# Interleaving the first two chunks of the second matrix, a convolution that ends later, and what moves with it

## What is computed

```python
def _conformer_layer(x, norm_g, w_in, dw_w, dw_b, ln_g, ln_b, w_out):
    h = _rms_norm(x, norm_g)
    u = h @ w_in
    a, b, z = jnp.split(u, 3, axis=-1)
    y = a * jax.nn.sigmoid(b)
    y = _depthwise_causal_conv(y, dw_w, dw_b)   # 31 taps
    y = jax.nn.silu(_layer_norm(y, ln_g, ln_b))
    y = y * jax.nn.silu(z)
    return x + y @ w_out
```

## Time and profile before

| | |
|---|---|
| median of 3 runs | 1309.73 us (1308.83 to 1312.35) |
| the profiled execution, its own time | 1308.54 us |
| its span, first to last instruction | 1306.7 us |
| PE busy | 1288.9 us, 99% |
| DVE busy | 827.2 us, 63% |
| ACT busy | 781.7 us, 60% |
| granted clock of TensorE | 0.998 |

### The profile page before, as it was taken

How to read it: one execution, slowest core, us unless ns; L and a number is a source line. 1 busy time by engine, 2 the same in 40 slices (tenths; PEclk the granted TensorE clock), 3 DMA queues, 4 the chain that set the end, 5 groups by cost and what they waited for, 6 DMA issues and landing times.

```text
span 1306.7 us, 16159 instructions
## 1 busy us (share of the span) xinstructions
PE 1288.9 (99%) x5987; PEld 1050.7 (80%) x5987; DVE 827.2 (63%) x1282; ACT 781.7 (60%) x1284; POOL 37.6 (3%) x88
## 2 busy tenths in 40 slices
PE   9999999999999999999999999999999999999997
PEld 7877777677888888888888887889888888888886
DVE  5789999977556665445666666555644445566545
ACT  6599998846547554444455665446845445566543
POOL 1011111100000000000000000000000000000000
PEclk9999999999999999999999999999999999999999
DMA  7599999955666556666554445665655556654563
GB/s 267 155 289 273 302 258 258 280 168 165 184 186 186 186 185 190 194 193 190 164 160 147 146 147 179 186 184 156 182 149 156 161 161 177 190 165 154 179 194 134
DMA packets 124789, 247.54 MB, mean 189 GB/s; under 512 B 7820, under 2 KB 12552, under 8 KB 124552
## 3 DMA queue, kind: packets, MB, share of 16 engines
q1 hardware_dynamic: 119496, 227.63, 55.5%
q0 software_dynamic: 5184, 18.88, 7.4%
q10 hardware_dynamic: 32, 0.01, 0.0%
HBM read 225.51 MB, written 2.10 MB: 174 GB/s over the span
## 4 chain that ended last, share of the span: by engine, by line
PE 88%; ACT 6%; DVE 3%; DMA 2%; issue 1%; SPq 0%; DVEq 0%; ACTq 0%
PE PS L1449 26%; PE PS L1451 26%; PE PS L1450 26%; PE PS L1437 3%; PE PS L1370 3%; ACT tap_products L903 2%; ACT w_hi L487 2%; PE PS L1384 2%; DMA tap_products<-tap_products 1%; ACT L468 1%; DVE w_lo L937 1%; DVE aux L1058 1%; DMA w_raw<-in_a_w_in 1%; DVE heads_out L1261 1%; ACT stage L545 0%
## 5 line engine op out<-in xcount | busy, mean ns | idle before, releaser
L937 DVE TENSOR_TENSOR w_lo<-w_raw,w_hi 128x1024 fp32r<-128x1024 f32 (+2 forms) x406 | 490.3, 1209 | 395.2 <-ACT w_hi L487 393.9
L487 ACT ACTIVATE w_hi<-w_raw 128x1024 fp32r<-128x1024 f32 (+2 forms) x406 | 423.7, 1047 | 401.9 <-PE PS L1451 383.8
L1449 PE MATMUL PS<-w_hi,actA_hi 128*128 128x512 f32 (+1 forms) x856 | 340.8, 398 | 4.5 <-DVE w_lo L937 3.1
L1451 PE MATMUL PS<-w_hi,actA_lo 128*128 128x512 f32 (+1 forms) x856 | 332.1, 388 | 0.0
L1450 PE MATMUL PS<-w_lo,actA_hi 128*128 128x512 f32 (+1 forms) x856 | 331.5, 387 | 0.0
L1449 PE MATMUL PS<-w_hi,actB_hi 128*128 128x512 f32 (+1 forms) x768 | 305.0, 397 | 0.0
L1451 PE MATMUL PS<-w_hi,actB_lo 128*128 128x512 f32 (+1 forms) x768 | 297.3, 387 | 0.0
L1450 PE MATMUL PS<-w_lo,actB_hi 128*128 128x512 f32 (+1 forms) x768 | 296.5, 386 | 0.0
L1449 PEld LDWEIGHTS PS<-w_hi,actA_hi 128*128 128x128 f32 x856 | 160.7, 188 | 41.8 <-issue 8.9
L1450 PEld LDWEIGHTS PS<-w_lo,actA_hi 128*128 128x128 f32 x856 | 160.9, 188 | 34.0 <-issue 3.3
L1451 PEld LDWEIGHTS PS<-w_hi,actA_lo 128*128 128x128 f32 x856 | 160.7, 188 | 32.8
(11 more groups left out here) (235 smaller groups left out, 778.1 us busy)
## 6 DMA issues: line engine op xcount, KB each, us to landing
w_raw<-in_a_w_in SPq DMA_DIRECT2D x96, 512.0 KB, 6.7
w_raw<-in_w_in SPq DMA_DIRECT2D x88, 512.0 KB, 3.7
w_raw<-in_w_kv SPq DMA_DIRECT2D x64, 512.0 KB, 3.8
w_raw<-in_b_w_in SPq DMA_DIRECT2D x64, 512.0 KB, 3.7
tap_products<-tap_products POOLq DMA_DIRECT2D x36, 512.0 KB, 8.1
w_raw<-in_a_w_out SPq DMA_DIRECT2D x32, 512.0 KB, 3.9
w_raw<-in_b_w_out SPq DMA_DIRECT2D x32, 512.0 KB, 3.8
w_raw<-in_w_out SPq DMA_DIRECT2D x32, 512.0 KB, 4.2
```

The costliest lines, as they stand in the source:

```text
L487: nc.scalar.activation(split_slot(u)[0], w_raw[:, RAW_SLOT[u], 0:2 * w], ACT.Copy)\
L937: V.tensor_tensor(wl, w_raw[:, RAW_SLOT[u], 0:2 * w], wh.bitcast(F32), ALU.subtract)\
L1449: T.matmul(bank, ah, wh[:, kk, :], start=first and kk == 0, stop=False)
L1451: ins = T.matmul(bank, al, wh[:, kk, :], start=False, stop=last and kk == 1)
```

## The change

It does these things:

- The first two chunks of the second matrix share units 96 to 111: two units of chunk 12, two of 13, and so on. Quarter g of the input is so first needed by unit 96 + 4g. Chunk 12 is done at unit 110, chunk 13 at 112 (`DONE`, `JUST_DONE`), and their residual sums and transposes move there.
- Ten plain units in place of 17: 21, 35, 46, 53, 55, 64, 76, 82, 87, 89.
- The convolution runs from unit 19 to 89, the transposes for statistics at 43, 62, 77, 90. 37 pairs in place of 36, at other taps; an addition at least 4 steps behind its pair; 5 buffers for sums and 3 for addends, in the room of 4 x 2. The transposes and copies of y are one step earlier.
- Mean and root in step 90, normalisation in 92, 93, 99, 102, the products with silu(z) in 93, 96, 100, 103, with high and low halves one step behind each. Z's third chunk is evacuated in step 89, and the last two wait in the room of y.
- The rotary tables are made in steps 166 to 171.
- The ring of loads is wide from unit 16 on.

```diff
+n = UNITS.index((C_OUT, 0))
+UNITS[n:n + 16] = [(C_OUT + c, 2 * g + i) for g in range(4) for c in range(2) for i in range(2)]
+DONE = [max(u for u, (c, _) in enumerate(UNITS) if c == n) + 1 for n in range(NCH)]
+JUST_DONE = {u: c for c, u in enumerate(DONE)}
...
-WIDE_FROM, WIDE_TO = 20, 100
+WIDE_FROM, WIDE_TO = 16, 100
...
-CONV_FROM = [20, 36, 52, 68]
+CONV_FROM = [19, 35, 51, 67]
...
+PLAIN = {21, 35, 46, 53, 55, 64, 76, 82, 87, 89}
+WHOLE = [u in PLAIN for u in range(NU)]
...
-PAIRS, IN_FLIGHT = 9, 4
+PAIRS, SUMS, ADDENDS = [9, 10, 9, 9], 5, 3
...
-CONV_TO = 88
+CONV_TO = 92
+ACT_LEAD, DVE_LEAD, PAIR_LAG = 0, -5, 4
...
-            if added < len(made) and made[added] + 3 <= u and taken[added // PAIRS]:
+            if added < len(made) and made[added] + PAIR_LAG <= u and taken[j]:
...
-                STATS_AT.append(u + (2 if j == 3 else 4))
+                STATS_AT.append(u + (1 if j == 3 else 4))
...
-MOMENTS_AT = STATS_AT[3] + 1
-NORM_AT = [89, 91, 93, 95]
-Z_EVAC_AT = [73, 80, 93, 96]
-Z_AT = [92, 94, 97, 100]
+MOMENTS_AT = STATS_AT[3]
+NORM_AT = [MOMENTS_AT + at for at in (2, 3, 9, 12)]
+Z_EVAC_AT = [73, 80, 89, 96]
+Z_AT = [93, 96, 100, 103]
+ROPE_AT = FIRST[C_V] + 6
...
         def pair_products(n, i):
-            return tap_products[:, n % IN_FLIGHT, i, :, :]
+            return tap_products[:, SUMS + n % ADDENDS if i else n % SUMS, :, :]
...
+                if u == SQUARES_AT[1] + 1:
+                    want(SIGMOID)
+                if u == ROPE_AT + 3:
                     want(EXP_LN)
...
-                    want(SIGMOID)
+                    table[0] = None
...
-                if s == 4 and 2 <= c <= C_Z and c % 2 == 0:
+                if s == 3 and 2 <= c <= C_Z and c % 2 == 0:
...
+                if u == MOMENTS_AT - 2:
+                    want(EXP_LN)
                 if u == MOMENTS_AT:
                     guess("ln")
+                    want(SILU)
...
-                    if n >= IN_FLIGHT:
-                        act.wait_ge(S["product_added"], n - IN_FLIGHT + 1)
+                    if n >= SUMS:
+                        act.wait_ge(S["product_added"], n - SUMS + 1)
+                    if n >= ADDENDS:
+                        pair_summed(act, n - ADDENDS)
...
-                    gated_parts(f"z{j}", conv, 4 * j, "B", 4 * j,
-                                lambda: dve.wait_ge(S["silu_ready"], j + 1))
+                    transposed(dve, f"z{j}")
+                    dve.wait_ge(S["silu_ready"], j + 1)
+                    for i in range(2):
+                        a = conv[:, 4 * j + 2 * i:4 * j + 2 * i + 2, :]
+                        V.tensor_tensor(a, bank_pair(i), a, ALU.mult).then_inc(S["t_multiplied"], 1)
+                if u - 1 in Z_AT:
+                    j = Z_AT.index(u - 1)
+                    for i in range(2):
+                        hi_bank()
...
+                if C_OUT <= JUST_DONE.get(u, 0) < C_K:
+                    add_residual(JUST_DONE[u], "x1_ready")
...
-                if s == 3 and 2 <= c <= C_Z and c % 2 == 0:
+                if s == 2 and 2 <= c <= C_Z and c % 2 == 0:
```

More of the change, by code:

```diff
@@ L105, in plan_convolution @@
         act_at, dve_at = act_at + ACT_ELSE[u], dve_at + DVE_ELSE[u]
-        while len(made) < 4 * PAIRS and act_at < pe_at:
-            j, m = divmod(len(made), PAIRS)
-            if u < CONV_FROM[j] or len(made) - added >= IN_FLIGHT:
+        while len(made) < PAIR_FROM[4] and act_at < pe_at + ACT_LEAD:
+            j = max(i for i in range(4) if PAIR_FROM[i] <= len(made))
+            if u < CONV_FROM[j] or len(made) - added >= SUMS:
                 break
-            PAIRS_AT[u].append((j, m))
+            PAIRS_AT[u].append((j, len(made) - PAIR_FROM[j]))
             made.append(u)
@@ L113, in plan_convolution @@
         act_at = max(act_at, pe_at - 30)
-        while dve_at < pe_at and added + sum(taken) < 4 * (PAIRS + len(SOLO_TAPS)):
-            if added < len(made) and made[added] + 3 <= u and taken[added // PAIRS]:
-                CONV_OPS[u] += [(added // PAIRS, "add", added % PAIRS, i) for i in (0, 2)]
+        while dve_at < pe_at + DVE_LEAD and added + sum(taken) < PAIR_FROM[4] + sum(len(t) for t in SOLO_TAPS):
+            j = max(i for i in range(4) if PAIR_FROM[i] <= added)
+            if added < len(made) and made[added] + PAIR_LAG <= u and taken[j]:
+                CONV_OPS[u] += [(j, "add", added - PAIR_FROM[j], i) for i in (0, 2)]
                 dve_at, added = dve_at + 12, added + 1
@@ L119, in plan_convolution @@
             open_taps = [i for i in range(4) if u >= CONV_FROM[i]
-                         and taken[i] < len(SOLO_TAPS) - (added < (i + 1) * PAIRS)]
+                         and taken[i] < len(SOLO_TAPS[i]) - (added < PAIR_FROM[i + 1])]
             if not open_taps:
@@ L123, in plan_convolution @@
             j = open_taps[0]
-            CONV_OPS[u] += [(j, "tap" if taken[j] else "first", SOLO_TAPS[taken[j]], k) for k in range(4)]
+            CONV_OPS[u] += [(j, "tap" if taken[j] else "first", SOLO_TAPS[j][taken[j]], k) for k in range(4)]
             dve_at, taken[j] = dve_at + 16, taken[j] + 1
-            if taken[j] == len(SOLO_TAPS):
-                STATS_AT.append(u + (2 if j == 3 else 4))
+            if taken[j] == len(SOLO_TAPS[j]):
+                STATS_AT.append(u + (1 if j == 3 else 4))
         dve_at = max(dve_at, pe_at - 30)
-    assert added == 4 * PAIRS and sum(taken) == 4 * len(SOLO_TAPS), (added, taken)
+    assert added == PAIR_FROM[4] and [len(t) for t in SOLO_TAPS] == taken, (added, taken)
 plan_convolution()
-MOMENTS_AT = STATS_AT[3] + 1
-NORM_AT = [89, 91, 93, 95]
-Z_EVAC_AT = [73, 80, 93, 96]
-Z_AT = [92, 94, 97, 100]
+MOMENTS_AT = STATS_AT[3]
[3 more added lines that the diff above has]
+ROPE_AT = FIRST[C_V] + 6
 SPLITS = []
@@ L667, in _ @@
                         transposed(act, "y3")
[L668 to L672 removed]
+                    if j == 2:
+                        act.wait_ge(S["conv_ready"], 3)
+                    evacuate(C_Z + j, z_stage(j), ACT.Silu, r_x)
+                if u - 1 in Z_AT:
+                    j = Z_AT.index(u - 1)
                     for i in range(2):
@@ L677, in _ @@
                         ins.then_inc(S["t_hi_ready"], 1)
-                if s == 2 and C_OUT < c <= C_K:
-                    j = c - C_OUT - 1
+                if C_OUT <= JUST_DONE.get(u - 2, 0) < C_K:
+                    j = JUST_DONE[u - 2] - C_OUT
                     transposed(act, f"w{j}")
@@ L1044, in _ @@
             tap_done = {}
-            ops_left = [4 * len(SOLO_TAPS) + 2 * PAIRS for _ in CONV_FROM]
+            ops_left = [4 * len(SOLO_TAPS[j]) + 2 * PAIRS[j] for j in range(4)]
             refined = {}
```

70 lines of the change are left out of this document (38 added, 32 removed).

## The result

| | before | after |
|---|---|---|
| median, same chip | 1310.71 us (1308.83 to 1312.35) | 1299.05 us (1298.15 to 1300.06) |
| ratio of the times | | 0.9912, 95% interval 0.9895 to 0.9929 |
| the profiled execution | 1308.54 us | 1300.06 us |
| its span | 1306.7 us | 1298.2 us |
| PE busy, DVE busy, ACT busy | 1288.9, 827.2, 781.7 us | 1283.5, 832.7, 795.5 us |

By the ratio the change gains 11.5 us (9.3 to 13.8); between the two profiled executions it is 8.5 us. The forecast was 1300.5, with -9.2 us. I go by the spans of the traces for where the time went, and come back to the difference of 3 us at the end.

The account below looks back on a forecast made before the run. PE, busy in every slice, was taken as the bound: its instructions plus the places where it stands still. -5.0 (plain units) - 5.2 (three stalls) + 1.0 (new ones) = -9.2 us, so 1300.5 against 1309.73; range 1298 to 1305.5.

Parts of the forecast that it names:

- Seven plain units: Plain units 17 to 10: seven units go from 3.43 to 2.72 us each, 5.0 us less on PE.
- third stall: PE's wait before the transposes feeding the last statistics (unit 90): 1.72 us, forecast to go with 0.4 us to spare.
- Three stalls: PE waits on DVE between unit 16 and the second matrix: 1.09, 2.38 and 1.72 us, all forecast to go, -5.2.
- ready at about start(86), plus 9.13: Last pair sum's landing; with 1.21 and 1.58 more, 11.9 us, against PE reaching unit 90 at 12.3 us.
- New stalls: New PE waits, 1.0 us: 0.5 at y's transposes and addend buffers, 0.5 for everything outside the convolution.
- rotary move: Rotary tables made in steps 166 to 171 instead of 14 to 16: nothing on PE at either place.
- wider ring: Wide ring of loads from unit 16: load 16 held back until unit 13, nothing on PE, 2.5 us to spare.
- A: Convolution: DVE still the bound, stalls return elsewhere or seven splits cost DVE their saving; 1304.7 us, chance 0.17.
- B: Chain from the last statistics misses unit 90 or 96; 2.7 us more, 1303.2 us, chance 0.10.
- C: Slower: DMA engines are the bound, pair sums landing beyond 10.9 us; at 11.5 us 22 us more, 1322, chance 0.05.
- D: The skill page's 1.38 us drain per table switch delays q's transposes by 1.4 us; 1301.9 us, chance 0.03.
- E: At the start, load 16 shares engines with five more; PE stands still some 4.5 us; 1305 us, chance 0.05 with the unnamed.

## Why the prediction was right, and where it was not

**Seven plain units, -5.0.** 80 records, and the two kernels that differ in seven such units alone are 3.4 us apart in span, 5.0 once the third stall is counted out. The room for them had to be there: in the kernel before seven more splits lose 3.4 to 7.1 us. Counting each engine's work over the stretch gave the right sign both times (0.6 us of slack and a loss, 5.2 and a gain).

**Three stalls, -5.2.** With seventeen plain units all three go and the span is 5.1 us shorter. In the changed kernel the first two go, 3.5 us. A lag of four alone takes away 3.4 of the 5.2 in the kernel before: 3.47 for those two, less 1.10 for two others that come, and 1.0 of the third. The third stayed in the changed kernel. The step that failed is "ready at about start(86), plus 9.13": I followed the last pair sum and gave it 0.4 us to spare, and took for granted that DVE and its splits were on time. What ended last was the load of the weights of unit 91, on a queue that I had passed over in this part, though a split that waits 2.78 us for its load stands in the earlier trace rows. The stall's size changes from execution to execution, 0 to 1.67 us, with the landing of that load. The load is that late only with whole pair sums and with the slot of plain unit 82 held, as the table shows for one execution of each kernel; with either gone it takes 5.3 to 9.6 us instead of 12.0 to 13.6. What that is worth in the medians is too small to be told. And a late load is not the only way to this stall: with nine plain units DVE's work alone leaves 0.8 us of it.

**New stalls, +1.0.** 0.45 us: 0.23 at unit 24 and 0.22 at the queries' transposes, where I had 0 to 0.2. The first is not shown to come from the change, since both experiments on the kernel before have one of 0.23 and 0.21 at unit 23 (77.6 and 77.8 us) as well. Y's transposes, unit 96 and the later chunks cost nothing. The rotary move and the wider ring, for which I put nothing on PE, save 0.7 and 0.5 us of stalls by one trace each; the medians can't tell these.

**The sum.** By the changed kernel's trace: -5.0 - 3.5 + 0.45 + 0.3 (a later start, before any unit of the convolution) = -7.8, and the span gives -8.5; 0.7 us I can't place. It lies between units 16 and 96, and about 0.3 of it are steps of PE that were a little long in the trace before. Against my terms the third stall is 1.7 us too much and the new ones are 0.55 too little, and so the forecast of the span, -9.2, was near by two misses that partly cancel.

**The rivals.** A did not come: the stalls did not come back, with room for them and the lag of four. The run with a lag of three shows that it was near: 6.6 us. B did not come, nor C: sums land 7.7 us after their issue in the median, before 8.1. D: as in the earlier trace rows, the instruction behind a table load starts at its end (270.64 + 1.28, and the evacuation at 271.93), and so it is behind 22 of the trace's 25 loads; the other three instructions waited for DVE or a DMA. With the 0.22 us at the queries' transposes, the 1.38 us of drain that the Trainium skill gives ("ScalarE: Activation LUTs", section "What ACT_TABLE_LOAD costs") are not paid in this kernel. E: the split of unit 16 waited 3.06 us for its load and PE didn't wait for it.

**The difference between 8.5 and 11.5 us.** I stood on one profiled execution of the kernel before, and it was 2.2 us under the median beside which the change was measured; the changed kernel's was 1.0 us above its own. The 2.22 us of idle time in the earlier trace rows explain this best: in other executions of the kernel before they may be as long as the 2.52 us that were followed by a fallen clock with ten plain units, and then cost 1.6 us more. For it speak the granted clocks. Of the 27 executions of the kernel before beside the experiments, 19 have a mean clock of 0.997 or 0.996, and those at 0.996 are 2.0 us longer in the mean than those at 0.998 (1311.7 and 1309.7). None of the 49 executions of the kernels whose trace has no idle time over 2.1 us is below 0.998. Some 3.3 us at half the clock lower the mean by 0.0013, though a stretch at half the clock at the end of every trace, 2.5 to 5.7 us long, moves it by as much. A lag of four alone, which takes that stall away, also gains 2 us more by the medians than by the spans. It stays an inference: no trace of the kernel before with a fallen clock was taken.

## What to carry to other kernels

When a helper engine is full, give the asynchronous step between two of its tasks more distance before you give the engine more work: one step of lag was worth 3 us by itself, and 6.6 us once the room had been used for something else (by the medians 5.0 and 7.1). Slack summed over a stretch told the sign of the change here, twice, but not its size, since single waits of 2 us reached the bound engine however much slack lay elsewhere. For the last task of a chain follow every input back to its issue, the weight loads too, and not only the one that was late before.
